# Expert weights of a two-layer decoder: every load in 2 KB runs, issued as soon as its place is free

## What is computed

```python
def swiglu(x, w_gate, w_up, w_down):
    return (jax.nn.silu(x @ w_gate) * (x @ w_up)) @ w_down

def moe_swiglu(h, router_w, w_gate, w_up, w_down):
    ...
    top_val, top_idx = lax.top_k(logits, TOP_K)
    gates = jax.nn.softmax(top_val, axis=-1)
    combine = jnp.einsum("nk,nke->ne", gates, jax.nn.one_hot(top_idx, N_EXPERTS, dtype=jnp.float32))
    y = jnp.zeros((B * T, D), dtype=jnp.float32)
    for e in range(N_EXPERTS):
        y = y + combine[:, e:e + 1] * swiglu(xt, w_gate[e], w_up[e], w_down[e]).astype(jnp.float32)
```

## Time and profile before

| What | us |
|---|---|
| median of three runs | 1593.9 |
| the profiled execution | 1592.3 |
| its span in the profile | 1590.5 |
| TensorE busy (PE) | 1514.3 |
| weight loads busy (PEld) | 1328.0 |
| VectorE, ScalarE, GpSimd busy | 258.1, 179.0, 143.4 |

### The profile page before, as it was taken

How to read it: one execution, slowest core, us unless ns; L and a number is a source line. 1 busy time by engine, 2 the same in 40 slices (tenths; PEclk the granted TensorE clock), 3 DMA queues, 4 the chain that set the end, 5 groups by cost and what they waited for, 6 DMA issues and landing times.

```text
span 1590.5 us, 54507 instructions
## 1 busy us (share of the span) xinstructions
PE 1514.3 (95%) x25957; PEld 1328.0 (83%) x25957; DVE 258.1 (16%) x489; ACT 179.0 (11%) x383; POOL 143.4 (9%) x167
## 2 busy tenths in 40 slices
PE   8999999999999999999999999999999999999997
PEld 7787587777687864888999999999998899999996
DVE  3433410000243434100010010010000010000002
ACT  3223220000131332200000000000000000000001
POOL 2243200000022522200000000000000000000000
PEclk9999999999999999999999999999999999999999
DMA  9213344444242145999999999999999999999992
GB/s 338 87 53 133 106 159 159 159 159 146 103 149 107 54 154 189 353 373 356 383 384 371 377 361 377 384 371 371 376 372 366 357 372 382 371 374 361 387 370 95
DMA packets 133612, 433.48 MB, mean 273 GB/s; under 512 B 9082, under 2 KB 33916, under 8 KB 119052
## 3 DMA queue, kind: packets, MB, share of 16 engines
q1 hardware_dynamic: 132384, 427.70, 71.8%
q0 software_dynamic: 672, 2.14, 0.5%
q10 hardware_dynamic: 332, 0.13, 0.0%
HBM read 428.89 MB, written 1.05 MB: 270 GB/s over the span
## 4 chain that ended last, share of the span: by engine, by line
PE 92%; issue 3%; DVE 2%; ACT 1%; POOL 1%; DMA 0%; ACTq 0%; DVEq 0%
PE ps L1126 35%; PE ps L1150 18%; PE ps L975 9%; PE ps L681 8%; PE ps L986 4%; PE ps L844 4%; PE ps L692 3%; PE ps L1183 2%; PE ps L1055 1%; PE ps L801 1%; PE ps L811 1%; PE ps L707 1%; PE ps L714 1%; PE ps L677 1%; PE ps L821 1%
## 5 line engine op out<-in xcount | busy, mean ns | idle before, releaser
L1126 PE MATMUL ps<-AT_sb,ring 128*64 128x88 f32 x5376 | 216.6, 240 | 13.2 <-issue 13.0
L1150 PE MATMUL ps<-LT_sb,ring 128*64 128x88 f32 x5376 | 215.9, 239 | 13.0 <-issue 12.3
L1126 PEld LDWEIGHTS ps<-AT_sb,ring 128*64 128x64 f32 x5376 | 210.7, 138 | 19.0 <-issue 17.0
L1126 PE MATMUL ps<-wpost,ring 128*64 128x88 f32 x5376 | 215.1, 239 | 11.4 <-issue 10.1
L1150 PEld LDWEIGHTS ps<-LT_sb,ring 128*64 128x64 f32 x5376 | 210.8, 137 | 17.4 <-issue 14.9
L1126 PEld LDWEIGHTS ps<-wpost,ring 128*64 128x64 f32 x5376 | 209.7, 138 | 16.3 <-issue 13.5
L975 PEld LDWEIGHTS ps<-hT_sb,ring 128*128 128x128 f32 x768 | 136.0, 190 | 24.6 <-issue 9.1
L975 PE MATMUL ps<-hT_sb,ring 128*128 128x256 f32 (+1 forms) x768 | 155.7, 362 | 0.0
L681 PE MATMUL ps<-hT_sb,ring 128*128 128x256 f32 x592 | 133.4, 383 | 0.0
L681 PEld LDWEIGHTS ps<-hT_sb,ring 128*128 128x128 f32 x592 | 112.4, 192 | 15.9 <-DVE late L1628 0.5
L1972 POOL TENSOR_SCALAR small<-small 128x1 f32<-128x1 f32 x16 | 3.8, 240 | 1196.6 <-ACT late L1506 927.2
(11 more groups left out here) (284 smaller groups left out, 1144.7 us busy)
## 6 DMA issues: line engine op xcount, KB each, us to landing
ring<-in_moe_w_gate SPq DMA_DIRECT2D x84, 1024.0 KB, 8.3
ring<-in_moe_w_up SPq DMA_DIRECT2D x84, 1024.0 KB, 8.1
ring<-in_moe_w_down SPq DMA_DIRECT2D x84, 1024.0 KB, 8.1
late<-in_moe_w_up SPq DMA_DIRECT2D x28, 1024.0 KB, 8.2
late<-in_moe_w_gate SPq DMA_DIRECT2D x28, 1024.0 KB, 7.9
late<-in_moe_w_down SPq DMA_DIRECT2D x28, 1024.0 KB, 8.2
ring<-in_ffn_w_gate SPq DMA_DIRECT2D x11, 1024.0 KB, 5.3
ring<-in_ffn_w_up SPq DMA_DIRECT2D x11, 1024.0 KB, 8.0
```

The source lines that it names most:

```text
L1126: ins = mm(o[lo:lo + P // 2, :], pairs[:, m % 2, lo:lo + P // 2], xgT[e % 2][:, k, :], start=(k == 0 and m % 4 == 0), stop=(k == KD - 1), ...
L1150: ins = mm(o[lo:lo + P // 2, :], d[:, i, m * P + lo:m * P + lo + P // 2], moe_hid[:, 2 * j + i, :], start=(first and m % 4 == 0), stop=las ...
```

## The change

Every unit takes the form that the last chunk's gate and up units had: four blocks of 128 rows by 512 columns (`RUN`), four runs of 2 KB in each partition. In a chunk of 8 tiles a gate or up unit is now one half of the columns and four of the eight blocks of rows (`column_half`, `gate_ks`); a down unit is four blocks of rows and half of the 1024 columns. A partition then holds rows p, p + 128, ... of a down unit, so `pairs` goes, and the tiles are contiguous columns. The products of a unit go to one bank of PSUM (four tiles for each of four blocks of rows) where they went to two. The count of units, their places, the order of kinds and TensorE's 32 products on each stay.

The wait for `page_turn`, the marks, `pe_order`, `page_turns` and `turned` are taken out. A unit from the 17th on waits for `unit_used` alone.

```diff
-PAGE = 256
-FIRST_IN_PAGE = 67
-TURN_MARKS = (8,)
...
-PAGE_TURNS, UNIT_TURN = page_turns()
+RUN = 512
...
+        def column_half(c, j):
+
+            return j % 2 if MOE_TILES[c] == 8 else 0
+
         def gate_ks(c, j):
 
-            nk = 2 * 8 // MOE_TILES[c]
-            return range(j * nk, (j + 1) * nk)
...
+            first = j // 2 * 4 if MOE_TILES[c] == 8 else j * 4
+            return range(first, first + 4)
+
+        def unit_rows(n):
+            return unit_of(n).rearrange("p (r f) -> p r f", f=RUN)
...
                         sp_.wait_ge(unit_used, n - N_UNIT + 1)
-                        sp_.wait_ge(page_turn, UNIT_TURN[n - N_UNIT])
...
                     if kind == "d":
-                        lo = (MOE_AT[c] + 2 * j) * P
-                        dst = unit_of(n)
-                        src = moe_down[0, e][lo:lo + 2 * P, :].rearrange("(p i) d -> p (i d)", p=P)
+                        lo = (MOE_AT[c] + j // 2 * 4) * P
+                        src = moe_down[0, e][lo:lo + 4 * P, j % 2 * RUN:(j % 2 + 1) * RUN]
                     else:
-                        f = slice(MOE_AT[c] * P, (MOE_AT[c] + MOE_TILES[c]) * P)
+                        lo = MOE_AT[c] * P + column_half(c, j) * RUN
+                        f = slice(lo, lo + RUN)
                         ks = gate_ks(c, j)
-                        dst = gate_unit(n, c)
-                        src = (moe_gate if kind == "g" else moe_up)[0, e][ks.start * P:ks.stop * P, f]\
-                            .rearrange("(k p) f -> p k f", p=P)
-                    sp_.dma_start(dst, src).then_inc(unit_landed[n % N_UNIT], 16)
+                        src = (moe_gate if kind == "g" else moe_up)[0, e][ks.start * P:ks.stop * P, f]
+                    src = src.rearrange("(r p) f -> p r f", p=P)
+                    sp_.dma_start(unit_rows(n), src).then_inc(unit_landed[n % N_UNIT], 16)
...
-                        for m in range(MOE_TILES[c]):
-                            o = bank(b + m // 4)[:, m % 4 * SLOTS:(m % 4 + 1) * SLOTS]
-                            pairs = w[:, i, m // 2 * 2 * P:(m // 2 + 1) * 2 * P].rearrange("p (f i) -> p i f", i=2)
+                        for m in range(4):
+                            o = bank(b + hp)[:, m * SLOTS:(m + 1) * SLOTS]
                             for lo in (0, P // 2):
-                                ins = mm(o[lo:lo + P // 2, :], pairs[:, m % 2, lo:lo + P // 2],
-                                         xgT[e % 2][:, k, :], start=(k == 0 and m % 4 == 0), stop=(k == KD - 1),
+                                ins = mm(o[lo:lo + P // 2, :], w[:, i, m * P + lo:m * P + lo + P // 2],
+                                         xgT[e % 2][:, k, :], start=(k == 0 and m == 0), stop=(k == KD - 1),
                                          skip_group_check=True)
-                                turned(ins, e, f"{kind}{c}", call)
-                                call += 1
                     ins.then_inc(unit_used, 1)
...
-                    for i in range(2):
-                        first, last = c == 0 and j == 0 and i == 0, c == MOE_CH - 1 and j == MOE_TILES[c] // 2 - 1 and i == 1
-                        for m in range(KD):
-                            o = bank(4 + m // 4)[:, m % 4 * SLOTS:(m % 4 + 1) * SLOTS]
+                    for i in range(4):
+                        first, last = c == 0 and j < 2 and i == 0, c == MOE_CH - 1 and i == 3
+                        for m in range(4):
+                            o = bank(4 + j % 2)[:, m * SLOTS:(m + 1) * SLOTS]
```

More of the change, by code:

```diff
@@ L136, in page_turns @@
[L136 to L159, removed]
@@ L409, in build @@
         yT_act, yT_dve, yT_ps = (sem(n) for n in ("yT_act", "yT_dve", "yT_ps"))
-        page_turn = sem("page_turn")
         moe_acc = [sem(f"moe_acc{t}") for t in range(TT)]
@@ L1081, in gather @@
                     pe.wait_ge(ohT_ready, per_round(r, 1, N_EXP))
-                call = 0
                 for k in range(KD):
@@ L1086, in gather @@
                             ins = gather_part(j, k, t, n, t == 0 and n == 0, t == 1 and n == 2)
-                            turned(ins, e, "gather", call)
-                            call += 1
                     if k % 4 == 3:
@@ L1096, in onehot_transposes @@
                     ins = mm(bank(6)[0:SLOTS, t * P:(t + 1) * P], onehot[e % 2][:, t, :], ident_bf, start=True, stop=True)
-                    turned(ins, e, "oh", t)
                 ins.then_inc(ohT_ps, 1)
@@ L1113, in m_in @@
                 b = 0 if kind == "g" else 2
-                call = UNIT_CALLS * units_of(c, part)[0]
                 for j in units_of(c, part):
@@ L1117, in m_in @@
                     landed(r, n)
-                    w = gate_unit(n, c)
+                    w, hp = unit_rows(n), column_half(c, j)
                     for i, k in enumerate(gate_ks(c, j)):
@@ L1143, in m_down @@
                     landed(r, n)
-                    d = down_unit(n)
-                    for i in range(2):
-                        first, last = c == 0 and j == 0 and i == 0, c == MOE_CH - 1 and j == MOE_TILES[c] // 2 - 1 and i == 1
-                        for m in range(KD):
-                            o = bank(4 + m // 4)[:, m % 4 * SLOTS:(m % 4 + 1) * SLOTS]
+                    d = unit_rows(n)
+                    for i in range(4):
+                        first, last = c == 0 and j < 2 and i == 0, c == MOE_CH - 1 and i == 3
+                        for m in range(4):
+                            o = bank(4 + j % 2)[:, m * SLOTS:(m + 1) * SLOTS]
                             for lo in (0, P // 2):
                                 ins = mm(o[lo:lo + P // 2, :], d[:, i, m * P + lo:m * P + lo + P // 2],
-                                         moe_hid[:, 2 * j + i, :], start=(first and m % 4 == 0), stop=last,
+                                         moe_hid[:, j // 2 * 4 + i, :], start=(first and m == 0), stop=last,
                                          skip_group_check=True)
-                                turned(ins, e, f"d{c}", call)
-                                call += 1
                     ins.then_inc(unit_used, 1)
@@ L1164, in y_transposes @@
                     ins = nc.tensor.transpose(bank(6 + m // 4)[0:SLOTS, m % 4 * P:(m % 4 + 1) * P], yT[:, m, :], ident)
-                    turned(ins, e, "y", m)
                 ins.then_inc(yT_ps, 1)
@@ L1186, in scatter_piece @@
                              start=(quarter == 0), stop=True, skip_group_check=True)
-                    turned(ins, e, "s", 2 * i + n)
                 if quarter:
```

8 lines of the change are left out of this document (removed).

## The result

The changed kernel takes 1642.45 us (median of three runs, 1640.81 to 1646.79) against 1593.9 us: a ratio of 1.0307, with an interval of 1.0274 to 1.0339. The profiled execution took 1640.81 us with a span of 1639.0, 48.5 us more than before.

What follows compares the result with a forecast made beforehand. The DMA queue was taken as the bound, through the code fetch: loads end at 646.5 + 893 + 41 + 5 = 1585.5 us, plus 35 of tail, plus 1.8 and 1.6, gives 1624 us; range 1578 to 1655.

Steps and rivals of the forecast that it cites:

- The price of 2 KB runs: Expert stage's weight loads: every unit in 2 KB runs at 2.87 us, adding 41 us of queue time.
- Nothing hides this, since the engines are full: Step in pricing the expert stage's 2 KB runs: full DMA engines hide none of the 41 us added.
- The page waits: Expert-stage loads without SP's page-turn waits: of 21 us idle in the queue, 5 left, 16 won (ends 0 and 21).
- This can only fill what is idle in the queue: Step on SP's earlier issue of expert units: removing page waits can only use the queue's 21 us of idle.
- The tail: Time after the last weight landing: 35 us taken, between 18 and 50, where the kernel before had 30.
- some 90 us rather than 58: Sign of being right: TensorE's expert-stage idle stays "issue" in front of runs of 128, some 90 us rather than 58.
- cheap 2 KB runs: Rival on expert-stage loads: 2 KB runs cost no more than 4 KB, giving 1567 to 1584 us; chance 0.13.
- TensorE's own work: Expert-stage weight loads and matmuls: same number in another tile order, counted as nothing, bounds under 7 us.
- The quick fetch: Rival on TensorE's code fetch: 2 KB runs let it in sooner, tail 18 us, 1607 us in all; chance 0.20.
- The deep queue that holds each fetch longer: Rival on TensorE's code fetch: without pacing it waits 4.3 us in place of 2.9, 1660 us in all; chance 0.12.

Runs made afterwards that it cites:

- the later issues: Changed kernel where unit n waits for a unit moving from n - 16 at the start to n - 6 at the end: 1636.64 us, 1.0248 to before.
- mark 8: The kernel before, unchanged, with its page turn marked 8 instructions into a page: 1593.9 us.
- mark 240: Kernel before with the page turn marked at instruction 240 of the page before, 24 instructions earlier than at 8: 1714.59 us, ratio 1.0753.

## Why the prediction was right or wrong

The direction was right and 1642.45 us lies in the range, 18 us above the 1624 forecast. The way to it was only in part right, and that the number came near is luck in good part: the runs were priced at 41 us and cost some 6, the missing page waits at 11 us won (16 less 5 of tail) and cost 44.

**The price of 2 KB runs.** As a size of queue time it held: 51 us against 41 (ends 1 and 50), 2.91 us a unit against 2.87 (2.73 to 2.90), just past the upper end of both. What failed is the step "Nothing hides this, since the engines are full". With the turns kept, 36 us more of queue time made the kernel some 6 us slower. The sum itself had counted 21 us of idle in the queue, and gave them to the other part of the change.

**The page waits.** "This can only fill what is idle in the queue" is the step that was wrong. I priced the removal at 16 us won and 5 us more tail. Alone it costs 2.73%, which is 44 us. The pacing did not hold the loads back at a price; it set them behind the edges, so that of each pair about one unit was left when the next page was asked for (1.04 on the mean, against 1.23 to 1.24 without the turns). I had the evidence in front of me: the earlier trace rows show the fetch's wait as a matter of what is queued, and I used it for a rival and not for the sum. The queue of after did lose its idle (98.9% + 1.2%), but not for the reason of the forecast: with long runs and no turns 26 us stayed idle, so it is the 2 KB units that filled it, and it was worth nothing.

**The tail.** 49.5 us, the upper bound of 50 that I had worked out for places that fill again at once, where I took 35. The reason for the bound was right: the last issue of after stands at 1580.97 + 2.79 us, 55 us before the end, with some 14 units to go at the landing. But it is not a term: with the later issues it fell by 21 us, and the loads ended 14 us later.

**The form of the sum.** Loads' end plus tail takes the queue as the bound. It is TensorE that sets the end, at some 1530 us of work with its code in time, plus its idle. By that sum the forecast would have needed one number, the idle on "issue"; I named it as a sign ("some 90 us rather than 58"), and it came out at 99.4. (In the rival of cheap 2 KB runs one sum is off by 1, and nothing hangs on it: 646.5 + 893 + 10 + 5 is 1554.5, not 1555.5.)

**TensorE's own work.** Right: a load takes 137 ns in both lines, as the page's groups of after have it:

```profile
L1053 PEld LDWEIGHTS ps<-AT_sb,ring 128*64 128x64 f32 x5376 | 211.9, 137 | 20.3 <-issue 19.0
```

**The rivals.** Cheap 2 KB runs are out, at 2.91 us a unit. The quick fetch is out too: at the same pacing the fetch starts 2.68 us after the edge with 2 KB runs and 2.57 with long ones, not sooner. The Trainium skill, "DMA: Bandwidth & Descriptors", section "Queues, rings and completion order", has engines drain a whole packet before they turn to another queue. The trace agrees: with 33 packets of a unit on an engine (528 over 16), the code packet starts at the end of a unit's share in 79% of the pages of after, as with its 33 descriptors drained whole and not with a cut at 17. The deep queue that holds each fetch longer, to which I gave 0.12, had the mechanism. Its size was too large: it put every fetch 1.4 us later, while the mean moved from 2.57 to some 3.0 to 3.1 us, since only the pages with an issue close ahead of the edge pay in full. It had pages of 6.0 us; after's mean page takes 5.68 and before's 5.37.

What stays open: whether the code is asked for exactly at the edge or a little earlier (the marks at 8 and, 24 instructions sooner, at 240 bound it from both sides, and none between them was tried), and by which way 2 KB down units cost their few microseconds, the full queue or a fetch that starts a little later. No version here beats before.

## What to carry to other kernels

An engine that idles on "issue" at even distances may be waiting for its own code, which here came through the same DMA engines as the data; the packets of the instruction queue tell. Then neither a DMA share of 0.98 nor the place's wait on the loading engine tells what bounds the kernel: sum the idle on "issue" and see what is outstanding at each page's edge. A wait that looks like a brake on the loads may be what keeps them out of the code's way: here pairs of 1 MB loads cost least right behind the edge and most in the last two microseconds ahead of it. Try a change of pacing by itself before it is bundled with a change of size.

## What the runs showed of the hardware

- When the loads are issued, against the instruction pages of another engine, is worth up to 7.5% here: mark 8 gives 1594 us, mark 240 1715, with the same loads in the same order.
- A DMA queue can be full (after: 98.9% and 1.2%) or idle for a tenth of the time (mark 240: share 0.88), and neither says whether it is the bound. Leaving out half the bytes took 113 us off after's time, though TensorE never waited for a byte of weights.
- The code packet of 16 KB stands behind the units that are outstanding. It starts 1.0 to 1.3 us after the edge with little outstanding, 2.57 us on the mean of before and 4.2 us in the page of mark 240, and TensorE goes on 2.2 to 2.5 us after the packet starts (1023.3 to 1023.6, then 1025.81). Below some 2.5 us after the edge it costs nothing.
- 1 MB over 16 engines costs 2.91 us in 2 KB runs, beside 2.62 us in 8 KB and 2.79 us in 4 KB runs, 88 ns a packet (932.6 us x 16 / 169141).
